# Attention scores two heads at a time: 64-row matmuls on both halves of the array, unpadded keys, and four places for the weights

## The reference, cut to what matters

```python
s = jnp.einsum('bthd,btkhd->bhtk', q, k_sel) * (HEAD_DIM ** -0.5)
s = s - slopes[None, :, None, None] * dist[:, None]      # ALiBi
s = jnp.where(valid[:, None], s, -jnp.inf)
p = jax.nn.softmax(s, axis=-1)
o = jnp.einsum('bhtk,btkhd->bthd', p, v_sel)             # then o * silu(gate)
```

## Time and profile before

| | us |
|---|---|
| median of 3 runs (lowest, highest) | 2040.95 (2040.46, 2042.73) |
| the profiled execution | 2039.53 |
| its span | 2037.1 |
| TensorE busy in the span | 1791.7 (88%) |
| DVE, ACT, POOL busy | 1241.2, 580.9, 405.4 |
| the stage of the change, barrier to barrier | 577.6 to 766.6 |

### The profile page before, as it was taken

The page is one execution under the profiler, slowest core; times in us unless marked ns, Lnnn a source line. Parts: engine busy times, 40 slices in busy tenths (PEclk is TensorE's granted clock), DMA queues, the critical chain, the costliest instruction groups (busy, mean ns, idle before and its releaser), DMA issues. The chain is left out here.

```text
span 2037.1 us, 30876 instructions
## 1 busy us (share of the span) xinstructions
PE 1791.7 (88%) x11782; PEld 1046.2 (51%) x11782; DVE 1241.2 (61%) x2313; ACT 580.9 (29%) x1163; POOL 405.4 (20%) x385
## 2 busy tenths in 40 slices
PE   7999899999969998998379999999599877774977
PEld 4644554444446875473236666654254456662432
DVE  2034688889847665735594676767734345572387
ACT  0000550001145541211345555542131124341100
POOL 0101100001245541100001333320014302233120
PEclk9999999999979998979679999999799989897989
DMA  8414621221024007210842545442667377847301
GB/s 281 116 37 131 229 93 46 79 68 37 37 90 134 29 6 271 94 47 32 177 140 95 153 127 150 130 157 66 150 167 205 96 183 187 205 114 213 142 31 74
DMA packets 276288, 245.40 MB, mean 120 GB/s; under 512 B 132148, under 2 KB 229044, under 8 KB 275884
## 3 DMA queue, kind: packets, MB, share of 16 engines
q1 hardware_dynamic: 272884, 234.47, 39.2%
q0 software_dynamic: 3264, 9.02, 1.2%
HBM read 161.34 MB, written 86.63 MB: 122 GB/s over the span
## 5 line engine op out<-in xcount | busy, mean ns | idle before, releaser
L1868 PE MATMUL ri_ps<-ri_xm,od_w 128*128 128x384 f32 (+1 forms) x768 | 232.9, 457 | 0.1
L1893 PE MATMUL ri_ps<-od_w,ri_xm 128*128 128x512 f32 x512 | 227.8, 602 | 1.9 <-ACT od_big L2089 1.1
L1868 PEld LDWEIGHTS ri_ps<-ri_xm,od_w 128*128 128x128 f32 x768 | 145.0, 191 | 73.8 <-issue 2.4
L275 PE MATMUL ei_ps<-ev_w,ev_xT 128*128 128x512 f32 x384 | 168.6, 602 | 4.0 <-DMA ev_w<-in_e_w_in 4.0
L621 DVE TENSOR_SCALAR_CACHE_REDUCE ix_flags<-score,ix_cand 128x384 bf16<-128x384 f32 (+1 forms) x186 | 163.7, 942 | 12.2 <-DVE ix_cand L638 12.0
L543 PE MATMUL ix_ps<-ev_x,ev_xT 128*128 128x512 f32 x384 | 165.5, 593 | 0.0
L1893 PEld LDWEIGHTS ri_ps<-od_w,ri_xm 128*128 128x128 f32 x512 | 96.6, 192 | 117.8 <-issue 114.3
L1113 PE MATMUL go_psm<-go_w,qT 128*128 128x512 f32 (+1 forms) x288 | 134.1, 626 | 4.5 <-DVE qT L1256 4.2
L275 PEld LDWEIGHTS ei_ps<-ev_w,ev_xT 128*128 128x128 f32 x384 | 73.8, 193 | 96.8 <-issue 96.6
L543 PEld LDWEIGHTS ix_ps<-ev_x,ev_xT 128*128 128x128 f32 x384 | 72.7, 190 | 90.8 <-issue 90.8
L543 PE MATMUL ix_ps<-ev_w,ev_xT 128*128 128x512 f32 x256 | 110.4, 593 | 0.0
(11 more groups left out here) (330 smaller groups left out, 3034.7 us busy)
## 6 DMA issues: line engine op xcount, KB each, us to landing
ev_w<-in_e_w_in SPq DMA_DIRECT2D x5, 2048.0 KB, 10.4
scratch_h<-ix_qiT SPq DMA_DIRECT2D x40, 256.0 KB
od_w<-in_c_w_in SPq DMA_DIRECT2D x16, 512.0 KB, 5.7
od_w<-in_c_w_in SPq DMA_DIRECT2D x4, 2048.0 KB, 9.2
scratch_h<-ei_stage POOLq DMA_DIRECT2D x24, 256.0 KB, 2.3
ev_w<-scratch_h SPq DMA_DIRECT2D x3, 2048.0 KB, 18.9
ev_x<-in_e_w_in SPq DMA_DIRECT2D x3, 2048.0 KB, 26.7
go_uvg<-scratch_h SPq DMA_DIRECT2D x8, 768.0 KB, 6.8
```

The costliest lines, as they stand in the source:

```text
L275: last = nc.tensor.matmul(ps[n % NB][0:rows(t), 0:cw], xT[:, kd, t * P:t * P + rows(t)], rhs, start=(kd == 0), stop=(kd == KD - 1))
L1868: last = nc.tensor.matmul(out[:, 0:wd], w[:, ct % 2, kd, i * P:(i + 1) * P], xm[:, i, kd, lo:lo + wd], start=(kd == 0), stop=(kd == KD - 1))
L1893: last = nc.tensor.matmul(out[:], xm[:, j, kd, t * P:(t + 1) * P], w[:, a, kd], start=(kd == 0), stop=(kd == KD - 1))
```

## The change: what it does

The scores of heads 2c and 2c+1 are computed as two 64-row matmuls on the two halves of the array's rows, straight from `kT`; `at_kz`, its zeroing and its copies, and the waits for them are gone. TensorE's stream now goes by pairs of units: scores of u and u+1, then turn u-2, values of u-4, turn u-1, values of u-3. The scores of a pair wait until both units before are summed. `at_s` has four places. DVE does L855 and L858 of both units of a pair, and then the copies of the pair before; `finish` moves from head 2 to head 5. ACT and POOL keep their order.

```diff
-        s = sb("at_s", [P, 2, T])
+        s = sb("at_s", [P, 4, T])
-        kz = sb("at_kz", [P, H, T])
...
-            by_pair = kz[:].rearrange("p (c h) t -> p c h t", h=2)
-            for h in range(2):
-                nc.gpsimd.memset(by_pair[(1 - h) * HD:(2 - h) * HD, :, h], 0.0).then_inc(zeroed, 1)
-                pool.wait_ge(zeroed, h + 1)
...
-            pe.wait_ge(zeroed, 2)
...
-            for u, (i, h) in enumerate(units):
-                if u >= 2:
-                    pe.wait_ge(summed, u - 1)
-                if i == 0:
-                    pe.wait_ge(kz_v if h % 2 else kz_a, h // 2 + 1)
+            for u in range(0, len(units), 2):
+                i = units[u][0]
+                if u:
+                    pe.wait_ge(summed, u)
                 for s0, w in pieces(keys_of(i)):
-                    last = nc.tensor.matmul(ps_s[u % 2][:, s0:s0 + w], qT[:, h // 2, i * P:(i + 1) * P], kz[:, h, s0:s0 + w],
-                                            start=True, stop=True)
-                last.then_inc(qk, 1)
-                if u >= 1:
+                    for k in (u, u + 1):
+                        h = units[k][1]
+                        own = slice(h % 2 * HD, (h % 2 + 1) * HD)
+                        last = nc.tensor.matmul(ps_s[k % 2][:, s0:s0 + w], qT[own, h // 2, i * P:(i + 1) * P], kT[own, h // 2, s0:s0 + w],
+                                                start=True, stop=True)
+                        if s0 + w == keys_of(i):
+                            last.then_inc(qk, 1)
+                if u:
+                    turn_weights(u - 2)
+                    if u >= 4:
+                        attend_values(u - 4)
                     turn_weights(u - 1)
-                if u >= 2:
-                    attend_values(u - 2)
-            turn_weights(len(units) - 1)
-            attend_values(len(units) - 2)
-            attend_values(len(units) - 1)
+                    if u >= 4:
+                        attend_values(u - 3)
+            n = len(units)
+            turn_weights(n - 2)
+            attend_values(n - 4)
+            turn_weights(n - 1)
+            attend_values(n - 3)
+            attend_values(n - 2)
+            attend_values(n - 1)
...
-            for h in range(0, H, 2):
-                nc.scalar.copy(kz[0:HD, h], kT[0:HD, h // 2]).then_inc(kz_a, 1)
...
-            for h in range(1, H, 2):
-                nc.vector.tensor_copy(kz[HD:P, h], kT[HD:P, h // 2]).then_inc(kz_v, 1)
...
-                if u >= 2:
-
-                    dve.wait_ge(tr, last_tg[u - 2] + 1)
-                nc.vector.tensor_tensor_reduce(s[:, u % 2, 0:n], ps_s[u % 2][:, 0:n], bias[:, u % 2, 0:n], 1.0, -HUGE,
+                if u >= 4:
+
+                    dve.wait_ge(tr, last_tg[u - 4] + 1)
+                nc.vector.tensor_tensor_reduce(s[:, u % 4, 0:n], ps_s[u % 2][:, 0:n], bias[:, u % 2, 0:n], 1.0, -HUGE,
...
-                if u:
-                    copies(u - 1)
-                if h == 2 and i:
+                if u >= 3 and u % 2:
+                    copies(u - 3)
+                    copies(u - 2)
+                if h == 5 and i:
                     finish(i - 1)
+            copies(len(units) - 2)
             copies(len(units) - 1)
```

More of the change, by code:

```diff
@@ L693, in phase_attend @@
         go_in = sem("at_go_in")
-        zeroed, kz_a, kz_v = sem("at_zeroed"), sem("at_kz_a"), sem("at_kz_v")
         units = [(i, h) for i in range(NT) for h in range(H)]
@@ L761, in turn_weights @@
                     for j in range(m):
-                        last = nc.tensor.transpose(ps_t[n % 2][:, j * P:(j + 1) * P], s[:, u % 2, (k0 + j) * P:(k0 + j + 1) * P], ident[:])
+                        last = nc.tensor.transpose(ps_t[n % 2][:, j * P:(j + 1) * P], s[:, u % 4, (k0 + j) * P:(k0 + j + 1) * P], ident[:])
                     last.then_inc(tr, 1)
@@ L815, in _ @@
                 act.wait_ge(nmx_d, u + 1)
-                nc.scalar.activation(s[:, u % 2, 0:n], s[:, u % 2, 0:n], ACT.Exp, bias=nmx[:, u:u + 1],
+                nc.scalar.activation(s[:, u % 4, 0:n], s[:, u % 4, 0:n], ACT.Exp, bias=nmx[:, u:u + 1],
                                      accum_out=den[:, u:u + 1]).then_inc(exped, 1)
```

## The result

The changed kernel takes 2061.27 us (2058.53 to 2067.97 in 4 runs) against 2040.70 for the kernel before in the same comparison: ratio 1.0104, 95% interval 1.0079 to 1.0129, slower by 1%. Measured again later (e10) it was slower by 0.8%, 1.0051 to 1.0106. One execution of e10, with a granted clock of 0.59 over its span, took 3134 us and is in no ratio. I had forecast 2035.5, with a range to 2043. The profiled executions differ by 21.0 us (2060.56 and 2039.53). The stage took 189.0 us before, from its first DMA issue to the first of the next phase; now it takes 207.2 (575.8 to 783.0), not the 183.5 of the forecast. So 18.2 of the 21.0 are in the stage, and 2.8 in the rest of the program, which no edit touches.

What follows compares the result with a forecast made beforehand. TensorE was taken to bound the kernel, busy 167.9 of 182 us; the terms summed to -5.7, say -5.5 us, giving 2034.0 against the profiled execution and 2035.5 for the median, range 2031 to 2043.

Steps and rivals of the forecast that it cites:

- Scores side by side, the switch: TensorE's scores: two halves run together, removing 30.7 us; 0.09 a switch between 128-row and 64-row work, 6 us.
- The wait for the copies: Rounds from b = 5: the second turning waits for DVE's copies, 0.8 us a round, 20 us or so in all.
- Head: Start of the stage: zeroing and copies go, first sum at 582.9, not 587.17; -3.5 us.
- Tail: Last sum to last store: 16.3 us in place of 9.0; +7.3 us.
- The walk: TensorE's round and tail followed step by step with waits: 8.2 us a pair at b = 8, before 8.76.
- Tile 0's term: Tile 0, clock at half: TensorE's pair 2.1 us against 2.4, put at -1.6 us.
- -6.9: Tiles 0 to 3: b = 4 -2.6, b = 2 +1.0, b = 3 -1.0, tile 0 -1.6, lead-ins -2.7 us.
- -3.6: Rounds of b = 5 to 8, four pairs each: -2.2, -1.4, -0.6 and +0.6 us.
- +3.5: finish in rounds of b = 5 and up delays the next sum: about 4.5 us against 1 before.
- -2.5: Last period: the sums span 31.5 pairs before, 31 and the 1.35 within a pair after; 2.5 us less.
- a rival at 13%: The clock falls in TensorE's new waits, each fall costing 2 us; one a tile gives 2049 us; chance 13%.

Runs made afterwards that it cites:

- e10: The changed kernel run again, nothing altered, for a second profile: 2054.5 us, ratio 1.0078 to the kernel before.
- e2: The changed kernel's order, but scores as before (128 rows, padded keys, one head after the other): 2052.7 us, ratio 1.0045 to the kernel before.
- e5: The changed kernel with extra 128-row score matmuls where TensorE waits (head, first values, second turnings from b = 5, tail): 2049.9 us, ratio 1.0021.
- e7: e1's order with scores as in the kernel before (128 rows, padded keys, one head after the other): 2038.1 us, ratio 0.9982.
- e1: The changed kernel with values of u-4 before turning u-2 and values of u-3 before turning u-1: 2029.2 us, ratio 0.9939 to the kernel before.
- e11: e1 run again, nothing altered, for a second profile: 2029.8 us, ratio 0.9948 to the kernel before.
- e9: e1 with the scores of tiles 0 to 2 as in the kernel before (128 rows, padded keys): 2028.2 us, ratio 0.9940 to the kernel before.
- e8: e3 with a second, unread 64-row matmul on the other row half beside each score matmul in tiles 0 to 3: 2056.2 us in one run.
- e4: The changed kernel with 9 extra 128-row score matmuls in the tail: 2059.8 us, ratio 1.0078 to the kernel before.
- e6: e1 with four extra score matmuls at the head: 2036.1 us, ratio 0.9963 to the kernel before.
- e3: The kernel before, old order, with each head's scores by one 64-row matmul from unpadded keys, not side by side: 2192.3 us, ratio 1.0691.

## Why the prediction was wrong

The stages side by side (us, from the profiles):

| order | padded, 128 rows | side by side |
|---|---|---|
| old | 189.0 | |
| pairs, turning first (the change) | 197.7 (e2) | 207.2, 195.6 (e10); clock held 191.2 (e5) |
| pairs, values first | 181.6 (e7) | 174.8 (e1), 172.7 (e11); small tiles padded 170.1 (e9) |

- *Scores side by side, the switch.* Right: pairs of records 1.99 us for eight, couples at 8.0 for 8.2. The switch is 0.10 a time: from the last four score records of a round (two at a time) to the first turning are 0.96 us, where two times 0.43 are 0.86; and e8 shows that it has no hand in the clock. The two rows, after (start, duration):

```profile
741.92 1.02 PE L780 MATMUL at_pss<-kT,qT 64*128 64x512 f32 x4
742.88 0.33 PE L754 MATMUL at_pst<-go_ident,at_s 128*128 128x128 f32 x1
```

- *The wait for the copies.* Right in place and size (18.9 us; 1.21 in the round shown). e1 takes two thirds of it out by order alone: 6.4 us in 8 waits are left, the longest 1.5.
- *Head.* Right: the first sum 5.2 us after the stage began (580.95 less 575.8), forecast 5.3; before 9.6.
- *Tail.* The walk was right for the upper clock (16.8 in e10), and wrong by 10.2 us where the clock was low.
- *A slip.* Tile 0's term is 4 x 0.3 = 1.2 by its own numbers, not 1.6. It changes nothing here.

Cut into four parts, the stage shows where the forecast was missed (us; the forecast is the part in the kernel before plus the terms of the prediction: -3.5 and -6.9 in the first row, -3.6, +3.5 and -2.5 in the second, +7.3 in the third; the first sum of tile 4 starts at 645.1 before and at 636.2 in the changed kernel):

| part | before | forecast | changed | e10 | e5, clock held |
|---|---|---|---|---|---|
| start to the first sum of tile 4 | 67.5 | 57.1 | 60.4 | 59.1 | 59.8 |
| tiles 4 to 7, to the last sum | 109.5 | 106.9 | 117.3 | 116.7 | 109.3 |
| last sum to last store | 9.0 | 16.3 | 26.5 | 16.8 | 19.1 |
| last store to the next phase | 3.0 | 3.0 | 3.0 | 3.0 | 3.0 |

- *The step that failed* is the one under all sums: every term of TensorE was priced at the clock of the kernel before, low in tile 0 and up from tile 1 on, so the change of the clock was put at nothing. I had the falls as a rival at 13%, at 2 us each. The runs show three things in its place.
  - *Falls in tiles 4 to 7.* About 24 us are at the lower level in either profile (56 x 0.21 / 0.50 in the first; 31 x 0.30 / 0.50 and 80 x 0.03 / 0.50 in e10). With the clock held (e5) this part is 109.3, fillers included, against 117.3 and 116.7: the falls cost 7 to 8 us, and with what the fillers take more, but not over 12, the half of 24. That is 2 us or a little more for each of the three or four, as the rival had priced them; I gave it too small a chance.
  - *The tail.* The clock fell ahead of it and stayed down to its end, 10.2 us; in e10 it did not. My rival had falls of 4 us each, and no long stay.
  - *The rise in the head.* It came at 597 before, 594 in e2, 592 in e7, 590 in e9, all with 128-row scores in the first tiles; with side-by-side scores at 609, 606 (e10), 609 (e1) and 605 (e11), but in e4 at 596 with a fall until 610, and 598 and 625 where the head was filled (e5, e6). To the first sum of tile 4 that is 2 to 3 us more than forecast.
- The change halved the time of the score work, the part of TensorE's work in which e3 and e8 show that rows at work count, and added waits behind which the clock fell (e1, e11: with a third of them left, one fall or none). Neither alone holds it down for long once it is up: e2 has waits and full-row scores, e1 side-by-side scores and few waits, and each had one fall of some 3 us. But e2's copy waits are also shorter than those of the change (11.4 us and 1.4 at most, against 18.9 and 2.4), so how much of its steady clock is rows and how much shorter waits is not shown.
- The Trainium skill (TensorE: Matmul & The Clock Gate, Part 1) says "the default state is throttled, and activity releases the throttle". e3 qualifies what activity is: its TensorE is listed at work for 321 of 327 us and stays at the lower level. Its advice to avoid idle gaps (Why this matters for your kernels) would not have warned of that, nor of the change's own waits, of which the longest was 2.4 us: it speaks of longer gaps.
- *The order's own price.* At the held clock the stage is 191.2 with fillers, about the 189.0 of before. Of the 7.9 above the 183.3 of the table, 2.8 are in the tail, where 2 of filler were expected, 2.7 in the head, and 2.4 in tiles 4 to 7, with a filler in each round. So the walk with its waits holds to 2.4 us in 107.
- Open: why the rise and the falls of the clock differ between executions of one program (the changed kernel, e10), and what the up to 9 us are by which the rest of the program differed between profiles.

## What to carry to other kernels

Side-by-side half-row matmuls saved time here only where the clock stayed up (e1 and e11 against e7): look at the granted clock of each stretch before halving its work, price the stage at both levels, and ask what brings the clock back once it is down. When an order is rewritten by pairs, walk one round with the buffers counted: here values before turnings, with no buffer more, took most of the copy wait out (18.9 us to 6.4) and turned 1% slower into 0.6% faster. Full-row scores in the first tiles brought the clock up 15 us sooner (e9 against e11) and made the stage some 3 us shorter, too little for the whole to show.

## What the runs showed of the hardware

- Two 64-row f32 matmuls on the two halves of the rows, 128 output columns each, into different banks, run together (eight records in 1.99 us where four took 1.94); a switch between 64-row and 128-row work costs 0.09 to 0.10 us.
- Rows at work count for the clock: 64-row scores one after another left TensorE at 1.2 GHz for 327 us of nearly unbroken work (e3), and the same with both halves at work came to 2.4 GHz 17 us after the first score (e8). Padding with zero rows, which looks like waste, kept the clock (0.95 in the stage before).
- One stream can stay at either level: that of half-row scores, turnings and values ran for 124 us at 2.4 GHz (e8, from tile 4 on, one run) and at 1.2 in the same tiles of e3, where it had begun at 1.2. The tail of turnings and values alone ran at 1.2 to its end in one execution of the changed kernel and at 2.4 in the other (e10), behind the same wait of 1.56 us. It does not always stay down in such work: in e3 the clock came up in it, at 907.
- Behind waits of 1.3 to 2.4 us the clock fell for 3 to 14 us at a time with side-by-side scores (the changed kernel, e10); behind copy waits of up to 1.4 us with full-row scores it fell once, for some 3 us (e2). TensorE was at work for 7.00 of 7 us in some of these falls (667 to 674).
